# A hybrid attention and RWKV-7 block: the attention half of an output slab multiplied between the steps of the recurrence

## The reference, cut to what matters

```python
def mixer_ab(u, ...):
    z = u @ w_in
    ya = diff_attention(qa, ka, va, lam, subln_g, lambda_init)   # ends in an rms norm by head
    yb = rwkv7_time_mix(zb, ...)                                 # ends in a norm by head, times a gate
    return concatenate([ya, yb], axis=-1) @ w_out                # 256 x 2048 by 2048 x 2048
```

## Time and profile before

| | us |
|---|---|
| median of 3 runs | 2555.52 |
| the runs | 2553.52 to 2556.78 |
| the profiled execution's own time | 2555.16 |
| its span, first to last instruction | 2553.4 |

### The profile page before, as it was taken

How to read it: one execution, slowest core, us unless ns; L and a number is a source line. 1 busy time by engine, 2 the same in 40 slices (tenths; PEclk the granted TensorE clock), 3 DMA queues, 4 the chain that set the end, 5 groups by cost and what they waited for, 6 DMA issues and landing times.

```text
span 2553.4 us, 31712 instructions
## 1 busy us (share of the span) xinstructions
PE 2489.6 (98%) x13463; PEld 2056.5 (81%) x13463; DVE 1428.8 (56%) x1555; ACT 1093.3 (43%) x1216; POOL 147.6 (6%) x171
## 2 busy tenths in 40 slices
PE   8999999999999999999998999999999999999998
PEld 6888778778888888888777977777888888888876
DVE  5556775665445545455556667656545444545564
ACT  5445432454434334334445445554434434334442
POOL 4001224000000000000000000000000000000100
PEclk9999999999999999999999999999999999999999
DMA  8556511546565555555553654356555565555543
GB/s 262 191 180 207 172 31 69 198 170 230 182 197 181 197 188 185 190 196 182 181 181 116 207 164 151 116 165 225 190 189 192 182 197 184 194 189 190 183 169 127
DMA packets 224850, 453.22 MB, mean 177 GB/s; under 512 B 7865, under 2 KB 16375, under 8 KB 223435
## 3 DMA queue, kind: packets, MB, share of 16 engines
q1 hardware_dynamic: 219165, 430.63, 50.7%
q0 software_dynamic: 3648, 17.54, 2.2%
q10 hardware_dynamic: 1902, 3.07, 0.4%
HBM read 445.52 MB, written 2.10 MB: 175 GB/s over the span
## 4 chain that ended last, share of the span: by engine, by line
PE 92%; DVE 4%; ACT 2%; DMA 1%; issue 1%; DVEq 0%; SPq 0%; ACTq 0%
PE psum L295 28%; PE psum L297 28%; PE psum L296 28%; PE psum L780 1%; PE psum L895 1%; DMA raw<-in_w_mlp_up 1%; PE psum L1699 1%; PE psum L1708 1%; DVE wlo L284 1%; DVE uTl L437 0%; PE psum L1035 0%; PE psum L1036 0%; PE psum L1037 0%; PE psum L415 0%; ACT uTh L435 0%
## 5 line engine op out<-in xcount | busy, mean ns | idle before, releaser
L284 DVE TENSOR_TENSOR wlo<-raw,whi 128x2048 fp32r<-128x2048 f32 (+1 forms) x408 | 937.7, 2305 | 730.2 <-ACT whi L279 729.6
L279 ACT ACTIVATE whi<-raw 128x2048 fp32r<-128x2048 f32 (+1 forms) x408 | 773.9, 1902 | 760.6 <-DMA raw<-in_w_mlp_down 328.6
L295 PE MATMUL psum<-whi,uTh 128*128 128x512 f32 (+2 forms) x2176 | 857.0, 394 | 20.0 <-DVE uTl L437 12.5
L297 PE MATMUL psum<-whi,uTl 128*128 128x512 f32 (+2 forms) x2176 | 844.5, 388 | 0.0
L296 PE MATMUL psum<-wlo,uTh 128*128 128x512 f32 (+2 forms) x2176 | 844.3, 388 | 0.0
L295 PEld LDWEIGHTS psum<-whi,uTh 128*128 128x128 f32 x2176 | 411.0, 189 | 109.8 <-issue 26.9
L297 PEld LDWEIGHTS psum<-whi,uTl 128*128 128x128 f32 x2176 | 411.2, 189 | 82.0
L296 PEld LDWEIGHTS psum<-wlo,uTh 128*128 128x128 f32 x2176 | 411.5, 189 | 80.3 <-issue 2.4
L295 PE MATMUL psum<-whi,hTh 128*128 128x512 f32 x1024 | 400.1, 391 | 0.0
L297 PE MATMUL psum<-whi,hTl 128*128 128x512 f32 x1024 | 398.6, 389 | 0.0
L296 PE MATMUL psum<-wlo,hTh 128*128 128x512 f32 x1024 | 398.4, 389 | 0.0
(11 more groups left out here) (355 smaller groups left out, 1405.0 us busy)
## 6 DMA issues: line engine op xcount, KB each, us to landing
raw<-in_w_mlp_up SPq DMA_DIRECT2D x128, 1024.0 KB, 5.4
raw<-in_w_mlp_down SPq DMA_DIRECT2D x128, 1024.0 KB, 5.0
raw<-in_ab_w_in SPq DMA_DIRECT2D x48, 1024.0 KB, 5.1
raw<-in_w_ple_gate SPq DMA_DIRECT2D x32, 1024.0 KB, 5.0
raw<-in_c_w_in SPq DMA_DIRECT2D x24, 1024.0 KB, 5.3
raw<-in_ab_w_out SPq DMA_DIRECT2D x16, 1024.0 KB, 5.2
raw<-in_c_w_out SPq DMA_DIRECT2D x16, 1024.0 KB, 5.1
raw<-in_c_w_in SPq DMA_DIRECT2D x12, 736.0 KB, 4.5
```

What stands on the lines that cost most here:

```text
L279: act.activation(whi[:, q, :, 0:n], raw[:, q, :, 0:n], ACT.Copy).then_inc(hi_ready, 1)
L284: dve.tensor_tensor(wlo[:, q, :, 0:n], raw[:, q, :, 0:n], whi[:, q, :, 0:n].bitcast(F32), ALU.subtract).then_inc(lo_ready, 1)
L295: pe.matmul(o, xh, hi, start=(q == 0 and k == 0), stop=False)
L297: last = pe.matmul(o, xl, hi, start=False, stop=(q == 3 and k == 3))
```

## The change

- The attention half of slab 0, chunks q = 0 and 1, leaves `out_pair_pe`. It becomes eight parts of six matmuls (`attention_part_pe(q, k)`), put between the steps of the recurrence, into banks 6 and 7. `out_pair_pe` begins with the attention half of slab 1, and the transposes of groups 2 and 3 stand further apart in it.
- The transposes of groups 0 and 1, with their copies on ACT and DVE, and the splits of chunks 0 to 3 move into the recurrence too.
- Attention's norm is done earlier: its squares on ACT behind the gates, its sum and root on DVE between steps of tile 0's levels, its scaling on POOL ahead of RWKV's.
- The second tile's two `gate_pe` move from behind levels 2 and 3 to the place ahead of level 1.
- `x_first_pe(1)` now waits for tile 1's last level. `y_last_pe(0)` moves ahead of it, the state's `s_first_pe(1)` ahead of `u_pe(2)`. Other banks for `level_d_pe(1)` and the state of block 2; `asq`, `NT`, `QT`, `MT` of tile 1 and the four chunks of `whi` have other addresses.
- SP no longer holds the four chunks of slab 0 until both norms are prepared: each waits for its own condition.

A split and the copies of the transposes of group 2 (L371) stand between the two now. The diff, cut:

```diff
+        def chunk(v, q, ks):
+            _, kc = OUT_CHUNKS[v][q]
+            pe.wait_ge(*mark("xT_lo", st, 2 * kc + 2))
+            pe.wait_ge(lo_ready, 4 * (base[st] + v) + q + 1)
+            return out_blocks_pe(pe, v, q, ks)
+
+        pe.wait_ge(sem("y_out"), 2)
+        chunk(0, 2, range(4)).then_inc(mm_used, 1)
+        chunk(0, 3, range(3))
+        T_pe(pe, st, src, ready, 2)
+        out_blocks_pe(pe, 0, 3, (3,)).then_inc(mm_used, 1)
+        T_pe(pe, st, src, ready, 3)
+        for q in range(4):
+            chunk(1, q, range(4)).then_inc(mm_used, 1)
...
+    def attention_part_pe(pe, q, k):
+        if k == 0:
+            pe.wait_ge(*mark("xT_lo", "ab_out", 2 * q + 2))
+            pe.wait_ge(lo_ready, 4 * base["ab_out"] + q + 1)
...
         gate_pe(pe, 0, 1, 4)
+        pe.wait_ge(sem("x_out"), 16)
+        gate_pe(pe, 1, 0, 5)
+        gate_pe(pe, 1, 1, 6)
         level_y_pe(pe, 0, 1)
-        pe.wait_ge(sem("rw_g"), 2)
+        pe.wait_ge(sem("rw_g"), 4)
         product_pe(pe, 1, 0)
...
         level_d_pe(pe, 0, 2)
-        gate_pe(pe, 1, 0, 0)
-        pe.wait_ge(sem("rw_g"), 3)
         level_y_pe(pe, 0, 3)
...
         decay_pe(pe, 1, 0)
         pe.wait_ge(sem("ex"), 8)
+        T_pe(pe, "ab_out", y_src("ab_out"), y_ready("ab_out"), 0)
         level_y_pe(pe, 0, 5)
...
         u_pe(pe, 0)
+        T_pe(pe, "ab_out", y_src("ab_out"), y_ready("ab_out"), 1)
         level_d_pe(pe, 1, 2)
...
         y_first_pe(pe, 0)
+        attention_part_pe(pe, 0, 0)
         level_y_pe(pe, 1, 5)
         y_state_pe(pe, 1)
+        attention_part_pe(pe, 0, 1)
         level_d_pe(pe, 1, 5)
+        y_last_pe(pe, 0)
+        attention_part_pe(pe, 0, 2)
 
         x_first_pe(pe, 1)
         x_state_pe(pe, 2)
-        y_last_pe(pe, 0)
-        u_pe(pe, 2)
         s_first_pe(pe, 1)
         s_state_pe(pe, 2)
+        attention_part_pe(pe, 0, 3)
+        u_pe(pe, 2)
+        attention_part_pe(pe, 1, 0)
+        attention_part_pe(pe, 1, 1)
         s_last_pe(pe, 2)
         y_first_pe(pe, 1)
+        attention_part_pe(pe, 1, 2)
         x_state_pe(pe, 3)
         y_state_pe(pe, 2)
         y_state_pe(pe, 3)
         u_pe(pe, 3)
+        attention_part_pe(pe, 1, 3)
         y_last_pe(pe, 1)
...
         level_y_dve(dve, 0, 3)
+        subln_sum_dve(dve, link)
         level_d_dve(dve, 0, 3)
+        subln_rms_dve(dve, link)
         product_dve(dve, 1, 1, 0)
...
-                    sp.wait_ge(sem("a_rms"), 1)
-                    sp.wait_ge(sem("gated_y"), 8)
...
+                            if j == 0:
+                                sp.wait_ge(*((sem("bonus"), 2), (sem("bon"), 1), (sem("partial"), 3), (sem("gated_y"), 8))[q])
```

More of the change, by code:

```diff
@@ L116, in build @@
     wlo = at("wlo", [P, 4, 4, W], F32R, 48)
-    whi = at("whi", [P, 4, 4, W], F32R, 80)
+    whi = [at(f"whi{q}", [P, 4, W], F32R, (96, 104, 80, 88)[q]) for q in range(4)]
     ident = at("ident", [P, P], F32, 112)
@@ L951, in out_keep_act @@
         for tt in range(TT):
-            square(act, bank[2 * (s % 2) + tt][:], ssq[:, tt, j:j + 1], *mark("m_sq", st, 2 * j + tt + 1))
+            square(act, out_bank(st, j, tt)[:], ssq[:, tt, j:j + 1], *mark("m_sq", st, 2 * j + tt + 1))
         for tt in range(TT):
-            last = act.activation(m[:, tt, j * W:(j + 1) * W], bank[2 * (s % 2) + tt][:], ACT.Copy)
+            last = act.activation(m[:, tt, j * W:(j + 1) * W], out_bank(st, j, tt)[:], ACT.Copy)
         last.then_inc(sem("m_out"), 1)
@@ L1012, in out_pair_pe @@
     def out_pair_pe(pe, st, src, ready):
[L1014 to L1038, removed]
@@ new lines, in out_blocks_pe @@
+    def out_blocks_pe(pe, v, q, ks):
+        j, kc = OUT_CHUNKS[v][q]
+        for k in ks:
+            for tt in range(TT):
+                o = out_bank("ab_out", j, tt)[:]
+                xh = uTh[:, 4 * kc + k, tt * P:(tt + 1) * P]
+                xl = uTl[:, 4 * kc + k, tt * P:(tt + 1) * P]
+                hi, lo = whi[q][:, k, :], wlo[:, q, k, :]
+                pe.matmul(o, xh, hi, start=(kc == 0 and k == 0), stop=False)
+                pe.matmul(o, xh, lo, start=False, stop=False)
+                last = pe.matmul(o, xl, hi, start=False, stop=(kc == 3 and k == 3))
+        return last
@@ L1703, in level_d_pe @@
     def level_d_pe(pe, tt, li):
-        b = LEVEL_BANK[tt]
+        b = LEVEL_D_BANK[tt]
         pe.wait_ge(sem(f"y1c{tt}"), li)
         for p, s_, h_ in lockstep():
-            last = pe.matmul(bank[b + 2 + s_][half(h_), p * CH:(p + 1) * CH], Y1[tt][half(h_), 8 * s_ + p, :],
+            last = pe.matmul(bank[b + s_][half(h_), p * CH:(p + 1) * CH], Y1[tt][half(h_), 8 * s_ + p, :],
                              TTi[half(h_), tt, 8 * s_ + p, :], start=True, stop=True)
@@ L1715, in x_first_pe @@
         pe.wait_ge(sem(f"made{tt}"), 3)
-        pe.wait_ge(sem(f"y1c{tt}"), 5)
+        pe.wait_ge(*((sem("y1c0"), 5) if tt == 0 else (sem("tt1"), 6)))
         pe.wait_ge(sem("mixed"), N_AB - R0)
         for p, s_, h_ in lockstep():
-            last = pe.matmul(bank[X_BANK[tt] + s_][half(h_), p * CH:(p + 1) * CH], NT[half(h_), tt, 8 * s_ + p, :],
+            last = pe.matmul(bank[X_BANK[tt] + s_][half(h_), p * CH:(p + 1) * CH], NT[tt][half(h_), 8 * s_ + p, :],
                              vv[half(h_), tt, head(p, s_)], start=(p == 0), stop=(tt + h_ == 0 and p == 7))
```

93 lines of the change are left out of this document (52 added, 41 removed).

## The result

| | us |
|---|---|
| before, median of 17 runs | 2553.91 |
| changed, median of 17 runs | 2561.32 |
| ratio | 1.0027, 95% interval 1.0020 to 1.0033 |
| in the second group of runs | 1.0020, 1.0011 to 1.0030 |
| forecast | 2560.0, range 2549 to 2566 |

The change made the kernel 0.2 to 0.3% slower, 5 to 7 us. The profiled execution is not a typical one: it took 2553.89 us, the fastest of the 17, at a mean granted clock of 0.994, where the others have 0.990 to 0.993. It shows the order of work, but not the time lost by most executions. That it is faster than the profiled execution of the kernel before (2555.16) comes from code that the change doesn't touch: behind 508 us its clock is missing for 10.0 us, (1 - granted clock) x time, against 13.4 there.

A forecast was written before the change was run, and what follows sets the result against it. PE was taken to bound the kernel, ending last for 92% of the span. Order +1.8, clock +2.5 and code +0.5 summed to 4.8 us on 2555.16, forecasting 2560.0 us, range 2549 to 2566.

The forecast's parts named there:

- the clock behind the recurrence: Two longer PE idle times ahead of groups 2 and 3 bring back reduced clock: +2.5 us, bounds 0 and 3.4.
- Step 1, the levels: Tile 0's levels: early gates, DVE's root and the wait for POOL make the recurrence start 4.3 us late.
- the sign that would have spoken against the prediction: At the recurrence's start: the prediction would be wrong if it began without the 4 us of delay.
- Step 2, the recurrence: Up to `x_state_pe(3)`: seven parts and group 1's transposes, less idle time filled, bring the shift to +12.5 us.
- the 1.0 us of other waits that were to close: PE's later idle moments in the recurrence, expected to be filled, about 1.0 us in all.
- The gaps for code: Two PE gaps in the recurrence, 1.17 and 0.43 us, beside four chunk loads; 1.6 us first credited as gone.
- the 0.5 charged back: Remaining loads in the recurrence still cause code gaps: 0.5 of the 1.6 us credited, bounds 0 and 1.6.
- Step 3, behind `x_state_pe(3)`: To the end of the first two output slabs, DVE's norm sets the end: 50.5 us instead of 61.2.
- The slower rival: Clock falls in the levels too: one more gives 2561.6 us, two with full code 2564.4; chance 0.38 including other longer waits.
- The rival by which the change does not do what it says: In the recurrence, parts wait for split or transposes, each wait stretching it by as much; no separate chance given.

The follow-up runs named there:

- the second group of runs: The changed kernel run again beside the kernel before and the follow-up kernels: ratio 1.0020, mean +5.2 us against the kernel before.
- the fillers: Changed kernel plus two unused 128x512 f32 matmuls ahead of each of levels 3 and 4 of tile 0: ratio 1.0013 to the kernel before.
- the gate: Changed kernel with one second-tile gate kept ahead of level 1 and the other moved back ahead of level 3: ratio 1.0001 to the kernel before.
- the kernel with early gates: Kernel before with only the second tile's two gates moved ahead of level 1: ratio 1.0000 to the kernel before.
- the two with one early step: Kernel before with only the two gates early, ratio 1.0000, and kernel before with only attention's norm early, ratio 0.9999.
- the fastest kernel: Changed kernel with all eight parts behind the recurrence, DVE's last scaling first, one gate ahead of each of levels 1 and 3: ratio 0.9973 to the kernel before.

## Why the prediction was right, and where it was not

The measured 2561.3 and 2559.7 lie inside the range and on either side of the forecast of 2560.0. Some of that closeness is luck. The forecast stood 4.5 us above a median of three runs of the kernel before, 2555.52, which in 17 runs came out at 2553.91; the measured differences are 7.4 us (6.8 between the means) in the first group and 5.2 in the second. And two terms of the sum were wrong, with errors that cancel: the clock behind the recurrence was charged 2.5 us and cost nothing, and more falls in the levels were left out of the sum, where they cost 2.0 us (by the fillers) to 3.5 us (by the gate).

- **Step 1, the levels: right in kind, the size by execution.** Gates +1.26 at level 1 (1.7 taken; two gates cost 3.44 us, not 3.96, as they follow one another without a change), +0.8 at level 3 (1.2), +2.3 behind the root (2.6), 0.41 for POOL (0.7), 2.45 at the recurrence (4.3). The last difference is the clock. The old fall at level 5 made the way from there to the next wait for DVE 7.64 us long, against 6.08 at full clock in the kernel with early gates. Here it came at level 4, where DVE's root covers all but 0.15 us of it. With the two falls at equal price the shift is about 3.9, an estimate (2.45 + 1.56 - 0.15). In the second group's profile, with two falls more in the levels, it is 4.5. So the sign that would have spoken against the prediction, a recurrence that starts without the 4 us of delay, is there in one profile (2.45) and not in the other (4.5).
- **Step 2, the recurrence: +9.8 between its start and `x_state_pe(3)`, 8.2 forecast.** Two terms were too small. The part costs 1.5 us and not 1.40, seven times 0.1. And of the 1.0 us of other waits that were to close only 0.27 did: those for DVE of 1.19, 0.28 and 0.75 us are still there with 1.22, 0.27 and 0.76. The gaps for code went as first reckoned, and the 0.5 charged back did not come: no "issue" gap is left there. That they were waits for code is still only argued.
- **Step 3, behind `x_state_pe(3)`: right.** 50.2 us against a forecast of 50.5. DVE's last scalings end 22.0 and 27.6 us behind the point (22.1 and 27.7 forecast), and PE waits for both, 2.83 and 1.64 us (2.9 and 3.3). Taking the parts out moved the point by 10.0 and 4.0 us.
- **Clock, +2.5 behind the recurrence: wrong.** The fall is there (0.50 at 473), behind the first wait and not the second, but it lies in the wait for DVE: the stretch behind it is 28.19 us long with and without it. The term should have been 0.
- **The slower rival was the missing part.** It placed further falls in the levels, since the gates no longer lie between the waits of 2 us. The means speak for it: 4.2 us more of clock missing, 3.9 less with the fillers, which bring 2.0 us of time, and 4.0 less with one gate back in its place, which brings 4.7, of which 1.2 is order. The profiles agree on the place: the six of kernels with both gates and the norm early and no filler miss 3.4 to 6.8 us of clock in the levels, 5.4 on average, the kernel before and the two with one early step 3.4, 3.4 and 0. One profile each doesn't settle it: with one gate back it is 3.4, 0 and 6.9. I had given it a chance as a case of its own; it belongs in the sum, in place of the 2.5.
- **How the loss divides stays open.** "4.2 us of clock and 1.0 of order" is what the columns say, but the changed kernel has costless falls, two in the first profile (3.4 us counted, 0.15 lost), and the falls of the kernel before cost nearly in full. So the new order by itself costs more than 1.0 and the clock less than 4.2.
- **What else stays open.** Neither the early gates nor the early norm alone lowered the mean clock. That both are needed, because only together they leave several waits of 2 us one behind the other, is argued and not shown; no run had both without parts and early transposes.
- **The rival by which the change does not do what it says** did not happen: no part waited for its split or transposes.

## What to carry to other kernels

Moving work into the idle moments of a dependent chain pays only as far as PE idles there; past that each piece delays the chain's end one for one (here 10.0 us for seven parts), and it takes the cover from whatever the other engines do behind it. Before moving work ahead, look for the next chain behind the point (here DVE's norm) and count how much of PE's work is left to hide it. A single execution's trace can't price falls of the clock: compare mean granted clocks over ten runs, look in the traces whether a fall lies in a wait and so costs nothing, and treat a sparse stretch that loses its last dense group as a risk of its own.

## What the hardware showed that was not expected

- The place where the clock falls differs from execution to execution of one kernel, and with it the time: the 17 runs of the changed kernel go from 2553.9 us at a mean clock of 0.994 to 2563.9 at 0.991.
- Every fall in the three stretches of all fourteen profiles is 1.7 us of clock or twice that. What it costs depends on who sets the end there: about 1.6 us at level 5 of the kernel before, 0.15 at level 4 of the changed one, nothing behind the recurrence.
- A wait does not settle whether the clock falls. It fell behind one of 2.2 us (ahead of level 4, 0.50 at 377), while one of 2.1 ahead of level 1 in the kernel before had no fall behind it, and the fastest kernel (median 2547.11) waited 2.21 us ahead of level 4 and 2.21 again ahead of `level_d_pe(0, 4)` at full clock.
- The gaps on PE for which nothing is waited ("issue") go with the way the four chunks are loaded. In the three profiles with the old way they are 1.6, 1.9 and 3.1 us in the recurrence up to `x_state_pe(3)`; the longer gap of each (1.17, 1.76 and 2.44 us) lies beside DMA at 382 to 389 GB/s, the shorter 1 to 2 us behind that load. In the eleven with the new way there is none up to that point. What PE waits for in them no run shows.
- With the filler, the two microseconds from 377 on are at full clock in the profiled execution, though it fell later, from 387 on:

```profile
377.00:379.00 2.00, 1.93 (x64) 1.93 (x64) 1.66 (x12) 0.00 (x0) 0.00 (x0) 1.00 0.03 8
```
